# Order and landing places of the first four projections of a gated recurrence

## The reference

```python
h = rmsnorm(x, mix_norm[l])
hq, hf, hi, hg, aq, ak, av, ga, gb = split(h @ w_in[l])      # hq, hf, hi, hg: 1024 columns each
f = lb + (1.0 - lb) * sigmoid(hf)                            # forget gate, 8 heads of 128
q_a = silu(hq)
k_a = 1.0 - f
v_a = hi
log_f = log(f)
o_a = hgrn2_chunk_scan(q_a, k_a, v_a, log_f)                 # S_t = diag(f_t) S_{t-1} + k_t v_t^T ; o_t = S_t^T q_t
...                                                          # o_a is normed and gated with silu(hg)
...                                                          # a dilated attention on aq, ak, av beside it
x = x + (sigmoid(ga) * y_a + sigmoid(gb) * y_b) @ w_out[l]
```

## Time and profile before

| what | before |
|---|---|
| time, median of 3 runs | 2658.0 us (2656.32 to 2658.15) |
| the profiled execution | 2656.82 us, its span 2655.0 us |
| granted TensorE clock | 1.00 throughout |
| TensorE busy | 2645.1 us |
| VectorE busy | 1967.1 us |
| ScalarE busy | 1427.8 us |
| GpSimd busy | 166.1 us |
| chain that ended last, share of PE | 94% |

### The profile page before, as it was taken

How to read it: one execution, slowest core, us unless ns; L and a number is a source line. 1 busy time by engine, 2 the same in 40 slices (tenths; PEclk the granted TensorE clock), 3 DMA queues, 4 the chain that set the end, 5 groups by cost and what they waited for, 6 DMA issues and landing times.

```text
span 2655.0 us, 42138 instructions
## 1 busy us (share of the span) xinstructions
PE 2645.1 (100%) x15660; PEld 2240.7 (84%) x15660; DVE 1967.1 (74%) x2660; ACT 1427.8 (54%) x2021; POOL 166.1 (6%) x98
## 2 busy tenths in 40 slices
PE   9999999999999999999999999999999999999999
PEld 8888888888888888888888888888888888888888
DVE  6777767777777876777776888567777769876676
ACT  5446565445446565544545767554454466765543
POOL 0000000000000000000000132000000012210000
PEclk9999999999999999999999999999999999999999
DMA  7556455655555545556555754546555665454553
GB/s 239 190 175 207 150 169 169 202 190 195 193 193 196 166 160 183 176 190 196 180 190 190 230 167 165 185 149 205 190 178 192 212 199 185 162 188 159 186 190 130
DMA packets 324380, 489.26 MB, mean 184 GB/s; under 512 B 17312, under 2 KB 204064, under 8 KB 324256
## 3 DMA queue, kind: packets, MB, share of 16 engines
q1 hardware_dynamic: 323968, 487.47, 56.0%
q10 hardware_dynamic: 288, 0.07, 0.0%
HBM read 478.02 MB, written 1.05 MB: 180 GB/s over the span
## 4 chain that ended last, share of the span: by engine, by line
PE 94%; DVE 2%; ACT 2%; issue 1%; DMA 0%; POOL 0%; SPq 0%; ACTq 0%; DVEq 0%
PE bank L371 48%; PE bank L573 22%; PE bank L571 12%; PE bank L476 5%; PE bank L941 2%; PE bank L984 1%; PE bank L390 1%; DVE w_low L333 1%; ACT w_high L328 0%; PE bank L976 0%; DVE log_decay L2040 0%; PE bank L1647 0%; POOL decay L2118 0%; PE bank L1167 0%; ACT log_decay L1802 0%
## 5 line engine op out<-in xcount | busy, mean ns | idle before, releaser
L333 DVE TENSOR_TENSOR w_low<-raw,w_high 128x2048 fp32r<-128x2048 f32 x435 | 1008.3, 2319 | 397.5 <-ACT w_high L328 397.1
L328 ACT ACTIVATE w_high<-raw 128x2048 fp32r<-128x2048 f32 x435 | 831.1, 1912 | 474.5 <-PE bank L571 243.0
L371 PE MATMUL bank<-w_high,xT_parts 128*128 128x512 f32 x2304 | 739.4, 395 | 0.0
L573 PE MATMUL bank<-xT_parts,w_high 128*128 128x512 f32 x2560 | 618.6, 391 | 0.0
L573 PEld LDWEIGHTS bank<-xT_parts,w_high 128*128 128x128 f32 x2560 | 472.1, 188 | 92.2
L371 PEld LDWEIGHTS bank<-w_high,xT_parts 128*128 128x128 f32 x2304 | 432.6, 188 | 89.9
L371 PE MATMUL bank<-w_low,xT_parts 128*128 128x512 f32 x1152 | 448.7, 389 | 0.0
L571 PEld LDWEIGHTS bank<-xT_parts,w_low 128*128 128x128 f32 x2560 | 334.5, 191 | 16.7
L571 PE MATMUL bank<-xT_parts,w_low 128*128 128x256 f32 x2560 | 339.4, 282 | 0.0
L668 ACT ACTIVATE siluT<-gateT 128x256 f32<-128x256 f32 x160 | 66.8, 417 | 407.3 <-DVE gateT L724 406.9
L371 PEld LDWEIGHTS bank<-w_low,xT_parts 128*128 128x128 f32 x1152 | 216.6, 188 | 42.6
(11 more groups left out here) (308 smaller groups left out, 2684.7 us busy)
## 6 DMA issues: line engine op xcount, KB each, us to landing
raw<-in_w_in SPq DMA_DIRECT2D x288, 512.0 KB, 4.6
raw<-in_ffn_w_in SPq DMA_DIRECT2D x176, 512.0 KB, 4.5
raw<-in_ffn_wd SPq DMA_DIRECT2D x88, 512.0 KB, 4.1
raw<-in_ffn_w_out SPq DMA_DIRECT2D x88, 512.0 KB, 4.1
raw<-in_ffn_wg SPq DMA_DIRECT2D x86, 512.0 KB, 3.8
raw<-in_ffn_wu SPq DMA_DIRECT2D x86, 512.0 KB, 4.7
raw<-in_w_out SPq DMA_DIRECT2D x32, 512.0 KB, 4.2
raw<-in_w_branch_a SPq DMA_DIRECT2D x16, 512.0 KB, 5.3
```

The costliest lines, as they stand in the source:

```text
L328: nc.scalar.activation(wh[slot][:], raw[slot][:], ACT.Copy).then_inc(high_done[slot], 1)
L333: nc.vector.tensor_tensor(wl[slot][:], raw[slot][:], wh[slot][:].bitcast(F32), ALU.subtract).then_inc(low_done[slot], 1)
L371: mm = pe.matmul(o[:, 0:n], x[:, rows], w[slot][:, col + j * n:col + (j + 1) * n], start=start and first, stop=stop and last)
L573: mm = pe.matmul(bank[:], wh[s][:, w], xhl[:, kt, :, :], start=kt == 0, stop=False, skip_group_check=True)
```

## The change

The four chunks are projected in another order: both halves of the gate, then both halves of the query. Each has a landing buffer and a semaphore of its own, so SP's waits for a buffer to be read are gone. The keys of half 0 are made in DVE's step 5 and those of half 1 in step 7, the scans run in steps 7 and 8, all eight logarithms in ACT's step 7, and the queries are copied in steps 8 and 10.

```diff
-CHUNKS2 = [HQ, HF, HQ + 512, HF + 512, HI, HI + 512, HG, HG + 512, AV, AV + 512,
+CHUNKS2 = [HF, HF + 512, HQ, HQ + 512, HI, HI + 512, HG, HG + 512, AV, AV + 512,
...
-        hland = [over(f"hg_turned{i}", [P, 4, 4, TT, 32], 82 + 4 * i) for i in range(2)]
+        hland = [over(f"hg_turned{c}", [P, 4, 4, TT, 32], kib) for c, kib in enumerate((82, 86, 90, 66))]
...
                 if u in (8, 10, 12, 14):
                     c = u // 2 - 4
                     sp.wait_ge(hsq_turned, at2(lay, 4, c + 1))
-                    if c == 2:
-                        sp.wait_ge(hq_out, at2(lay, 2, 1))
-                    if c == 3:
-                        sp.wait_ge(k_done, at2(lay, 2, 1))
-                        sp.wait_ge(lnf_done, at2(lay, 2, 1))
-                    squares_home(sp, hsq[c % 2], hland[c % 2], hT_in[c % 2])
+                    squares_home(sp, hsq[c % 2], hland[c], hT_in[c])
...
-                        func, dst = (ACT.Silu, ACT.Sigmoid)[c % 2], stg[c % 2]
+                        func, dst = (ACT.Sigmoid, ACT.Silu)[c // 2], stg[c % 2]
...
-                for hf, step in ((0, 4), (1, 8)):
+                for hf, step in ((0, 8), (1, 10)):
                     if u == step:
-                        act.wait_ge(hT_in[0], at2(lay, 128, 64 * (hf + 1)))
+                        act.wait_ge(hT_in[2 + hf], at2(lay, 64, 64))
...
-                for hf, step in ((0, 6), (1, 12)):
+                for hf, step in ((0, 7), (1, 7)):
                     if u == step:
                         if hf == 0:
                             act.preload_act_table_set(EXP_LN)
-                        act.wait_ge(hT_in[1], at2(lay, 128, 64 * (hf + 1)))
+                        act.wait_ge(hT_in[hf], at2(lay, 64, 64))
...
-                for hf, step, scan in ((0, 6, 6), (1, 11, 13)):
+                for hf, step, scan in ((0, 5, 7), (1, 7, 8)):
                     if u == step:
-                        dve.wait_ge(hT_in[1], at2(lay, 128, 64 * (hf + 1)))
+                        dve.wait_ge(hT_in[hf], at2(lay, 64, 64))
...
                     if c >= 2:
-                        dve.wait_ge(hT_in[c % 2], at2(lay, 128, 64))
+                        dve.wait_ge(hT_in[c - 2], at2(lay, 64, 64))
```

More of the change, by code:

```diff
@@ L314, in build @@
         rsr_in = sem("rstd_residues_in"); vres_in = sem("a_v_residues_in")
-        sec_T2 = sem("sec_T2"); hsq_turned = sem("hg_squares_turned"); hT_in = [sem(f"hg_turned_in{i}") for i in range(2)]; sec_out2 = sem("sec_out2"); sig_done2 = sem("sig_done2"); wTa_out = sem("wTa_out")
+        sec_T2 = sem("sec_T2"); hsq_turned = sem("hg_squares_turned"); hT_in = [sem(f"hg_turned_in{c}") for c in range(4)]; sec_out2 = sem("sec_out2"); sig_done2 = sem("sig_done2"); wTa_out = sem("wTa_out")
         rrow_done = sem("rrow_done"); rrow_out = sem("rrow_out"); turned_out = sem("turned_out")
@@ L1786, in mix2_act @@
                     a.then_inc(chunk_out2, 1)
-                for hf, step in ((0, 4), (1, 8)):
+                for hf, step in ((0, 8), (1, 10)):
                     if u == step:
-                        act.wait_ge(hT_in[0], at2(lay, 128, 64 * (hf + 1)))
+                        act.wait_ge(hT_in[2 + hf], at2(lay, 64, 64))
                         nc.scalar.activation(qT[:, 4 * hf:4 * hf + 4, :].rearrange("p h (t k j) -> p (h t) k j", t=TT, k=4),
-                                             hland[0][:].rearrange("p k h t j -> p (h t) k j"), ACT.Copy).then_inc(hq_out, 1)
-                for hf, step in ((0, 6), (1, 12)):
+                                             hland[2 + hf][:].rearrange("p k h t j -> p (h t) k j"), ACT.Copy).then_inc(hq_out, 1)
+                for hf, step in ((0, 7), (1, 7)):
                     if u == step:
@@ L1802, in mix2_act @@
                             a = nc.scalar.activation(own_decay(hd, 1)[:, 0].rearrange("p t (k j) -> p t k j", k=4),
-                                                     hland[1][:, :, h].rearrange("p k t j -> p t k j"), ACT.Ln,
+                                                     hland[hf][:, :, h].rearrange("p k t j -> p t k j"), ACT.Ln,
                                                      bias=lb[:, hd:hd + 1], scale=omlb[:, hd:hd + 1])
@@ L2028, in mix2_dve @@
                             a = nc.vector.tensor_scalar(kT[:, hd, :].rearrange("p (t k j) -> p t k j", t=TT, k=4),
-                                                        hland[1][:, :, h].rearrange("p k t j -> p t k j"),
+                                                        hland[hf][:, :, h].rearrange("p k t j -> p t k j"),
                                                         lbn[:, hd:hd + 1], omlb[:, hd:hd + 1], ALU.mult, ALU.add)
```

## The result

The changed kernel took 2662.75 us (median of 20 runs, 2661.61 to 2663.7) against 2657.98 for the kernel before (20 runs, 2656.32 to 2659.18). The ratio is 1.0018, with a 95% interval of 1.0012 to 1.0024: 3 to 6 us slower. The middle of this, 0.18%, lies just under the 0.2% that the prediction took as the bound of what can be told; all of the interval lies above 1, so the kernel is not faster. The profiled execution took 2663.14 us with a span of 2661.3.

A forecast was written before the change was run, and what follows sets the result against it. PE was taken as the bound (busy 2645.1 of 2655.0 us). New waits of 4.75 us a layer against 1.77 gave +3.0, +6.0 for two layers, on the 2658.0 median: 2664.0 us, range 2659.5 to 2667.5.

The forecast's parts named there:

- First logarithms 2.85 later: ACT, step 7: half 0's logarithms end 2.85 us later, behind `w_high` of unit 9 and its wait for PE.
- Keys 3.04 with POOL's collision: DVE, step 7: half 1's keys take 3.04 us because POOL's level 0 difference gets in among them.
- The wait behind unit 9: PE at level 0: DVE's products ready at 1504.57, wanted at 1501.73, a new wait of 2.9 us a layer.
- The waits behind 11, 13, 15: PE at levels 2, 4 and 6: further waits of 1.2, 0.35 and 0.3 us a layer.
- The last sum of the forecast: Level 6, behind unit 15: products ready at 1541.8, PE wants them at 1541.5, a wait of 0.3 us.
- The sum: PE's new waits of 4.75 us a layer against 1.77 before: +3.0 a layer, +6.0 for two layers.
- the first case of the forecast: All four new PE waits as summed: 2664.0 us, own range 2662.5 to 2666, chance 0.52.
- Edits at nothing: Saved table load in step 4 (1.28 us of ACT) and SP's dropped waits were claimed to change no time.
- POOL finds a gap later: At step 7's keys: they cost 1.5 us, level 0 ready 1.6 earlier; +2.8, 2660.8 us; shares chance 0.27.
- POOL ahead of `w_low`: At `w_low` of unit 11: POOL gets in first, later waits vanish; +2.3, 2660.3 us; shares chance 0.27.
- No new wait: Level 0 done by 1501.68 at DVE, 2.9 us earlier; old waits vanish: -3.5, 2654.5 us; chance 0.09.
- Worse: One more POOL-DVE collision before level 0 or 2: 2667.7 us in both layers, 2666 in one place; chance 0.12.

The follow-up runs named there:

- Early logarithms with POOL first: Changed kernel with half 0's logarithms in ACT's step 5, their scans in step 6, and DVE waiting for POOL's difference before `w_low` at levels 0, 2, 4: 2653.97 us.
- POOL first: Changed kernel with DVE waiting, after the products of levels 0, 2 and 4, for POOL's next difference before starting `w_low`: 2660.64 us; same wait in kernel before: 2657.9.
- first experiment: Changed kernel with only the keys and scans of half 1 put back to DVE's steps 11 and 13: 2657.17 us, ratio 0.9997 to the kernel before.
- early logarithms: Changed kernel with half 0's logarithms in ACT's step 5 and their scans in DVE's step 6, table set loaded for each half: 2656.36 us.
- the repetition: The changed kernel run once more, unchanged, to look at the wait and the granted clock: 2663.0 us in one run.
- eight more scans: Changed kernel with eight extra scans on DVE behind those of half 1 in step 8, results unread: 2668.27 us, ratio 1.0041 to the kernel before.

## Why the prediction held

**Bound and possible gain.** PE was the bound, and 1.77 us a layer was all there was to get. Early logarithms with POOL first got it back: 4.1 us measured for the 3.5 reckoned.

**First logarithms 2.85 later.** Forecast 1488.25, measured 1488.91 - 0.65 = 1488.26. The `w_high` of unit 9 and its wait for PE stand in front of them in ACT's rows; with the logarithms in step 5 the delay was gone.

**Keys 3.04 with POOL's collision.** Measured 2.94, and 2.87 to the next start where I had 3.12 with the memset; the memset cost nothing. POOL got in after the first key, as reckoned. This is nearly all of the 0.26 by which level 0 was ready earlier than forecast (1504.96 - 0.65 = 1504.31, forecast 1504.57).

**The wait behind unit 9.** Forecast 2.9, counted from where the level products would start. They would have started 0.55 behind 1501.84, as before (1501.18 to 1501.73), so the measured delay is 1505.01 - 1502.39 = 2.62; 2.41 of it is listed as idle. Of the 0.28 too much, 0.25 is the term of the keys; mechanism and place were right.

**The waits behind 11, 13, 15.** Forecast 1.2, 0.35, 0.3; listed in the second layer 1.32, 0.33, 0.20. In the first, the one behind unit 11 is missing, since PE itself was slower on the way there by 1.6 us (last section). The forecast had no such thing. That it costs little is luck: PE would have waited for 1.3 of it anyway. The missing wait is also 1.2 of the 2.5 us by which the waits on that line (7.0) stayed under the forecast (9.5); the wait behind unit 9, listed as 2.4 for 2.9 in both layers, is another 1.0, and the waits behind 13 and 15 are the rest. The last sum of the forecast, redone, gives 0.4 behind unit 15 and not 0.3.

**The sum.** Forecast +3.0 a layer. Measured from the 32-column matmuls behind unit 9 to the level products behind unit 15: 1541.67 against 1538.81, +2.9, in the first layer, and +2.8 between the same places of the second. The profiled executions differ by 6.3 in their spans: some 5.6 in the two layers and 0.65 ahead of them, where the change moves nothing. The medians differ by 4.8, with an interval of 3.2 to 6.4, which holds the 5.6 and the 6.0 forecast. The profiled execution of before lay 1.2 under its median, that of after 0.4 over it; that part of the 6.3 is scatter. So the first case of the forecast is the one that came about, at 2662.75 for 2664.0, and it ended just inside 0.2%: the sum was 1.2 too high against the medians. Of this the two layers of the trace account for 0.4 (5.6 for 6.0), in the main by the keys, and the rest can't be told from scatter. The prediction gave "slower by more than 0.2%" 0.50 and "the same" 0.48; on which side of that line a time 0.6 us from it would fall was not foreseen.

**Edits at nothing.** A table load is again followed by the next instruction 1.29 after its start (1487.62 to 1488.91), so the drain that the Trainium skill adds ("ScalarE: Activation LUTs", section "What ACT_TABLE_LOAD costs") shows in this trace neither before nor after; the measurement decides. Table load, SP's waits, buffers and the order of chunks cost and brought nothing (first experiment).

**Rivals.** "POOL finds a gap later" is refuted by POOL's start in the middle of the keys; "POOL ahead of `w_low`" by its 3.88 us, and, made so on purpose, gave 2660.64 where 2660.3 had been reckoned for it. Both of its layers together cost 2.2 us in the trace, for the 2.3 reckoned; the slower clock in most executions was in no sum. "No new wait" did not come about; it needed DVE 2.9 us earlier, and with the first logarithms and scans out of the way level 0 was ready 3.4 us earlier against PE, and the wait was gone. The time was then 2656.36 and not the 2654.5 of that case, since waits of 1.06 us a layer stayed behind the units 11, 13 and 15. "Worse" did not come about either: up to level 6 the rows show the collisions of POOL with DVE that the sum has, and no other.

## What to carry to other kernels

Before work is taken out of a place, ask what it costs there: the second keys cost nothing in step 11 and the scans in step 13 some 1.3 us of PE. Work taken out of a place where an engine is late has to go to a place where it is idle, and "earlier in the program" is not that place: count the engine's whole queue from the last event that cannot move up to the first result that the bounding engine needs. Before anything is moved ahead of such a result, move what already stands there into a real gap (here ACT's 3.5 us in step 5). Two engines that exclude each other should be given their order by a semaphore where the short chain through one of them feeds the other. Here that gained 2.1 us in the changed kernel, 2.4 with the early logarithms (2656.36 to 2653.97), and nothing in the kernel before, where the keys used the time that POOL lost, so the queue is to be counted again afterwards.

## What the hardware did that was not expected

After some of the waits the granted TensorE clock fell. The windows of the changed kernel, with PE, PEld, DVE, ACT and POOL busy (instructions), then the clock, DMA share and GB/s; first layer behind the wait, then the second:

```profile
1502.00:1505.00 3.00, 0.60 (x64) 0.49 (x56) 2.80 (x7) 0.65 (x1) 0.00 (x0) 1.00 0.72 220
1505.00:1510.00 5.00, 4.99 (x45) 4.04 (x46) 2.16 (x1) 1.06 (x2) 3.88 (x1) 0.66 0.55 141
...
2204.00:2209.00 5.00, 5.00 (x47) 4.14 (x34) 1.97 (x2) 1.32 (x3) 3.65 (x1) 1.00 0.58 156
```

In the first layer PE ran part of this stretch at the lower of its two levels, 1.2 GHz instead of 2.4 (a mean of 0.66 over the window); single wide matmuls then took up to 0.63 us instead of 0.39, and the two units behind the wait took 12.38 us (1505.40 to 1517.78) for 10.79 in the second layer. Here this ate the wait of 1.3 us behind unit 11 and half of that behind unit 13, so that from the 32-column matmuls behind unit 9 to the level products behind unit 15 the first layer took no longer than the second (40.48 and 40.47 us). An estimate of its price where no wait follows is the whole 1.6. It came again in the repetition, in the first layer alone (0.66 in the same window, 1.00 in the second layer). With eight more scans, behind waits of 4.93 and 4.94 us, it fell in both layers, to 0.64 and 0.50 over the 6 us behind; in the 6 us with most of the wait it was 0.79 in the first layer and 0.97 in the second.

With POOL first, two waits of the same 2.41 us were followed by 1.00 in the profiled execution. That execution is not typical. The mean granted clock over the whole execution, known for each, was 1.000 in four of the eleven (2658.97 to 2660.34 us), 0.999 in six (2660.46 to 2661.61) and 0.998 in the slowest (2662.69). All twenty executions of the changed kernel had 0.999. A mean does not tell where the clock fell, but as far as it tells, the same kernel has the fall in some executions and not in others. The six took 2660.8 us (median) and the four 2659.8: about 1 us, in a kernel where the wait behind unit 11 (0.3 us) cannot absorb the fall. What decides it after a wait of 2.4 us is open. In the six variants whose waits for the level products were at most 1.75 us, 66 executions, the mean clock was 1.000 in all but one: 0.999, in the slowest of the kernel before with POOL first (2659.78 us).
